# Differential attention in the first block: where the difference of the two softmaxes is formed

## The chip, the cores and the metric

One core of a Trainium2 chip runs the whole program. The metric is the device time of one execution in microseconds (us); the time of the kernel before is the median of three executions.

## The reference, cut to what matters

The model has two blocks one after the other on 256 tokens of width 1024, all in float32. The first block has two layers, each with a feed-forward part, a mixer (a convolution branch, a pooling branch and an attention branch side by side, joined by an output projection) and another feed-forward part. The second block has a Fourier and a window attention mixer and two mixture-of-experts layers. The change is in the attention branch of the first block's mixer, "differential attention": 4 heads, each with two sets of queries and keys (c = 0, 1), queries in blocks of 128, 256 keys.

```python
s = jnp.einsum("bqhcd,bkhcd->bhcqk", q_blk, k)
s = s - slopes[None, :, None, None, None] * dist
p = jax.nn.softmax(s, axis=-1)
a = p[:, :, 0] - lam * p[:, :, 1]
return jnp.einsum("bhqk,bkhe->bqhe", a.astype(v.dtype), v)
```

The output of each head then goes through an RMS norm (the sub-norm) and, beside the conv and pool branches, into the output projection. lam is one number per layer.

## The kernel before

The kernel is written by hand, engine by engine: each engine has its own program, in order, and they meet at counting semaphores. Weights come in panels of 1 MB: SP issues the loads into four raw slots, ACT rounds each panel to a high part (L1206), DVE forms the low part (L1705), and PE multiplies high and low parts in three products (L660, L661, L662). Matrix products outside of this are in plain f32.

The mixer of layer l is `mix1(l)`, which each of the three engines has in its own version. Its attention part is a loop over i = 0 to 7, which stands for query tile `qt = i // 4` and head `h = i % 4`; the text calls i "head i". Every engine runs the loop with a lag, so that while one engine deals with head i another deals with head i-1:

- PE: `scores(i+1)` (L837, two products of 256 columns with K=64), then `attend(i-1)`. attend waits for `a_ready`, transposes the two 128x128 halves of the difference `a1` into PSUM bank 1 (L846), signals `at_ready`, waits until ACT has copied the result to `at1`, and multiplies `at1` with the values `v1` (L851, the "second product"). At i = 1 the mean of the conv norm follows (L823), at i = 2 its variance (L829), at i = 7 the transposes of the attended rows of query tile 0 (`attended_T`, L862). Those of tile 1 follow behind the loop, then the output projection.
- DVE: `bias_and_max(i)` (L1990 adds the distance bias, L1994 takes the row maxima), then `weights(i-1)`: the reciprocals of the two row sums (L2003), the second one times -lam (L2005), `a1` = first exponentials times the first reciprocal (L2006), and `a1` += second exponentials times the scaled second reciprocal (L2008). A drain stands between dependent instructions. At i = 2 the conv norm is centred (behind the mean), at i = 3 normalised (behind ACT's root of the variance), at i = 5 the low part of the conv and pool outputs is formed (behind ACT's silu), at i = 7 the sub-norm of query tile 0 follows.
- ACT: `exps(i)` (L1384, two exponentials with row sums, into `p1`), then `weights_T(i-1)`, the copy of the transposed weights from PSUM to `at1` (L1390). At i = 3 the root of the variance (L1409) follows the copy, at i = 4 the silu and its rounding (L1416, L1420), at i = 7 the sub-norm's parts (L1394, L1396, L1398). Changes of the function cost a table load.

`p1`, `a1`, `at1`, `s1` and the statistics `m1` are double buffered by i % 2. `ident` is the 128x128 identity among the constants.

Elsewhere in the kernel, in the norms, PE transposes and scales rows by a product with a diagonal matrix: DVE makes the diagonal with `tensor_scalar(diag, ident, rs, rt, mult, mult)` in `diagonals` (L1773), and `norm_T` (L674) runs four products of 128x128 by 128 columns to each signal to ACT, whose first reader is L1252.

Of the kernel before, what the change touches and what calls it, by code (L numbers as in the profile page):

```python
# [22 lines left out]
ALU = mybir.AluOpType  # L23
# [7 lines left out]
P = 128  # L31
# [88 lines left out]
def build(nc, A, out):  # L120
# [9 lines left out]
    R0, R1, R2, R3 = 0, 4096, 4096 + 3072, 4096 + 3072 + 3456  # L130

    with ExitStack() as ctx:
        def sb(name, shape, dt=F32):
            return ctx.enter_context(nc.sbuf_tensor(name, shape, dt))

        def sem(name):
            return ctx.enter_context(nc.semaphore(name))
# [31 lines left out]
        ps = ctx.enter_context(nc.psum_tensor("ps", [P, 8, BANK], F32))  # L169
        psf = ps[:, :, :].rearrange("p b c -> p (b c)")  # L170

        def k(name):
            a, n = CA[name]
            return K[:, a:a + n]

        def w(a, n):
            return W[:, a:a + n]

        ident, tri, iota = k("ident"), k("tri"), k("iota")
# [58 lines left out]
        v1 = w(R3 + 4096, 1024).rearrange("p (t n) -> p t n", t=2)  # L238
        s1 = w(R3 + 5120, 1024).rearrange("p (b n) -> p b n", b=2)
        p1 = w(R0 + 2048, 1024).rearrange("p (b n) -> p b n", b=2)  # L240
        a1 = w(R0 + 3072, 512).rearrange("p (b n) -> p b n", b=2)
        at1 = w(R0 + 3584, 512).rearrange("p (b n) -> p b n", b=2)
        osq = w(R2 + 1024, 512)
        on = w(R2 + 1536, 512)
# [1 line left out]
        lam = sb("lam", [P, 8])  # L246
        m1 = sb("row_stats", [P, 2, 8])
# [147 lines left out]
        a_ready = sem("weights_ready")  # L395
# [80 lines left out]
        def slot(p):  # L476

            return w_hi[:, p % SPLIT, :], w_lo[:, p % SPLIT, :]
# [26 lines left out]
        def hi3(pair):  # L505

            return [v.rearrange("p (k n) -> p k n", k=KD) for v in pair]
# [5 lines left out]
        def T(a, n):  # L513

            return t_hi[:, a:a + n], t_lo[:, a:a + n]
# [141 lines left out]
        def _(pe):  # L657
            def product(dst, a, b, start, stop):

                pe.matmul(dst, a[0], b[0], start=start, stop=False)  # L660
                pe.matmul(dst, a[0], b[1], start=False, stop=False)  # L661
                return pe.matmul(dst, a[1], b[0], start=False, stop=stop)  # L662

            def at(pair, *idx):
                return [v[idx] for v in pair]
# [94 lines left out]
            def mix1(l):  # L760
                n = 4 * l + 1
                p = G0[f"in{l}"]
# [4 lines left out]
                for b in range(2):  # L767
                    pe.wait_ge(w_ready, p + b + 1)
                    for c in range(2):
                        for kk in range(KD):  # L770
                            if b == 0 and c == 0:
                                hT_wait(n, kk)
                            mm = product(ps[:, b, c * 256:(c + 1) * 256],
                                         at(hi3(slot(p + b)), slice(None), kk, slice(c * P, (c + 1) * P)),
                                         T(kk * 256, 256), kk == 0, kk == KD - 1)
# [8 lines left out]
                for grp in range(4):  # L784
                    r = 64 * (grp % 2)
                    for t in range(2):
                        mm = pe.matmul(ps[r:r + 64, 2, (grp // 2) * 256:(grp // 2) * 256 + 256],
                                       up[:, t, grp * 64:(grp + 1) * 64], band[:, t, grp, :],
                                       start=t == 0, stop=t == 1)
# [4 lines left out]
                for c in range(2):  # L794
                    for j in range(TAP_STEPS):
                        for q in range(4):
                            mm = pe.matmul(ps[32 * q:32 * q + 32, 1, c * SEQ:(c + 1) * SEQ], tapw[c][:, q, j, :],
                                           zrep[:, c, q, 4 * j:4 * j + SEQ], start=j == 0, stop=j == TAP_STEPS - 1)
# [4 lines left out]
                for c in range(2):  # L803
                    mm = pe.matmul(ps[:, 2, c * 256:(c + 1) * 256], pool_bd[:, l, c, :], dT[:, c, :],
                                   start=True, stop=True)
                mm.then_inc(pp_ready, 1)

                for i, src in enumerate((qn, kn)):
                    pe.wait_ge(qkn_ready, 2 * l + i + 1)
                    for t in range(2):  # L810
                        for h in range(4):
                            mm = pe.transpose(ps[:, 3 + 2 * i + t, h * P:(h + 1) * P],
                                              src[:, t * 512 + h * P:t * 512 + (h + 1) * P], ident)
# [28 lines left out]
                def attend(i):  # L842
                    qt, h = divmod(i, 4)
                    pe.wait_ge(a_ready, 8 * l + i + 1)
                    for t in range(2):
                        mm = pe.transpose(ps[:, 1, (i % 2) * 256 + t * P:(i % 2) * 256 + (t + 1) * P],  # L846
                                          a1[:, i % 2, t * P:(t + 1) * P], ident)
                    mm.then_inc(at_ready, 1)
                    pe.wait_ge(aT_ready, 8 * l + i + 1)
                    for t in range(2):  # L850
                        mm = pe.matmul(ps[:, (7, 0)[qt], h * P:(h + 1) * P], at1[:, i % 2, t * P:(t + 1) * P],  # L851
                                       v1[:, t, h * P:(h + 1) * P], start=t == 0, stop=t == 1)
                    mm.then_inc(o_ready, 1)
# [12 lines left out]
                for i in range(9):  # L866
                    if i + 1 < 8:
                        scores(i + 1)
                    if i >= 1:
                        attend(i - 1)  # L870
                    if i == 1:
                        mean()
                    if i == 2:
                        variance()
                    if i == 7:
                        attended_T(0)
# [821 lines left out]
        def _(dve):  # L1698
# [236 lines left out]
            def mix1(l):  # L1935
                p = G0[f"in{l}"]
# [60 lines left out]
                def weights(i):  # L1997

                    b = i % 2
                    dve.wait_ge(p_ready, 8 * l + i + 1)  # L2000
                    if i >= 2:
                        dve.wait_ge(at_ready, 8 * l + i - 1)
                    dve.reciprocal(m1[:, b, 4:6], m1[:, b, 2:4])  # L2003
                    dve.drain()
                    dve.tensor_tensor(m1[:, b, 6:7], m1[:, b, 5:6], lam[:, 5:6], ALU.mult)  # L2005
                    dve.tensor_scalar(a1[:, b, :], p1[:, b, 0:256], m1[:, b, 4:5], None, ALU.mult)  # L2006
                    dve.drain()
                    dve.scalar_tensor_tensor(a1[:, b, :], p1[:, b, 256:512], m1[:, b, 6:7], a1[:, b, :],  # L2008
                                             ALU.mult, ALU.add).then_inc(a_ready, 1)

                def sub_norm(qt):
                    dve.wait_ge(osq_ready, 2 * l + qt + 1)
# [16 lines left out]
                for i in range(9):  # L2029
                    if i < 8:  # L2030
                        bias_and_max(i)
                    if i >= 1:
                        weights(i - 1)
                    if i == 2:
                        centre()
                    if i == 3:
                        normalise()
                    if i == 7:
                        sub_norm(0)
                    if i == 5:  # L2040
                        dve.wait_ge(ys_hi, l + 1)
                        rest(t_lo[:, 2048:3072], ystage, t_hi[:, 2048:3072]).then_inc(ys_lo, 1)
# [587 lines left out]
```

## Time and profile before

| | before |
|---|---|
| median of 3 runs | 2835.4 us (2830.19 to 2836.94) |
| profiled execution, own time | 2835.73 us |
| its span, first to last instruction | 2833.9 us |
| mean granted TensorE clock | 0.905 |
| PE matmul, busy | 2350.8 us (83%) |
| DVE, busy | 1057.4 us (37%) |
| ACT, busy | 718.1 us (25%) |

The span is the time of the one execution that was profiled; what the device time has beyond it lies before the first and behind the last instruction. A busy time says how long an engine had an instruction in work. A granted clock of 1.00 means that TensorE ran at 2.4 GHz, 0.50 that it ran at 1.2 GHz, a value between them a mixture of the two over the stretch. The attention loops lie at about 309 to 358 us (layer 0) and 886 to 935 us (layer 1).

### The profile page before, as it was taken

The numbers are of one execution on the slowest core, as the hardware profiler recorded it, in microseconds if no ns is written. First come the engines' busy times: TensorE is split into PE (matmuls) and PEld (weight loads), VectorE is DVE, ScalarE is ACT, GpSimd is POOL, SyncE is SP. The second block draws the span as 40 slices with busy tenths as digits, with TensorE's granted clock in tenths as the row PEclk, the third lists the DMA queues.
The fourth block names the chain that finished last, engine by engine and source line by source line (L and its number), as shares of the span: only waits on it lengthen the run. The fifth ranks groups of instructions, "written<-read, shape, count | busy, mean of one in ns | idle before, by whom it ended". The sixth has DMA issues, their size and how long they took to land.

```text
span 2833.9 us, 35797 instructions
## 1 busy us (share of the span) xinstructions
PE 2350.8 (83%) x13958; PEld 1617.6 (57%) x13958; DVE 1057.4 (37%) x1634; ACT 718.1 (25%) x969; POOL 118.3 (4%) x209
## 2 busy tenths in 40 slices
PE   6999689999997699999678888886569578888885
PEld 5888488888885688887523333332545533333332
DVE  4555645565556355724601000001678500000011
ACT  3334433343344233522100000011335100001000
POOL 0001000000010000000010000001000010000000
PEclk9999789999998799999789998898779789889998
DMA  7765137767752377532279999999410289999997
GB/s 258 268 233 179 60 112 264 263 207 263 259 173 83 101 255 249 179 101 86 75 306 393 396 398 401 400 401 400 136 45 1 89 336 397 397 402 402 399 399 303
DMA packets 248615, 713.60 MB, mean 252 GB/s; under 512 B 24432, under 2 KB 163824, under 8 KB 195056
## 3 DMA queue, kind: packets, MB, share of 16 engines
q1 hardware_dynamic: 213584, 642.82, 61.2%
q10 hardware_dynamic: 25936, 43.20, 4.4%
q0 software_dynamic: 8976, 25.90, 3.1%
q8 instruction: 88, 1.44, 0.2%
q14 instruction: 31, 0.25, 0.0%
HBM read 688.45 MB, written 25.26 MB: 252 GB/s over the span
## 4 chain that ended last, share of the span: by engine, by line
PE 57%; DMA 26%; DVE 7%; issue 3%; ACT 2%; DVEq 2%; SPq 1%; ACTq 1%; POOL 0%; POOLq 0%
DMA raw<-in_w 24%; PE ps L660 13%; PE ps L661 12%; PE ps L662 12%; PE ps L1009 11%; PE ps L674 2%; PE ps L701 2%; DMA shift_cols<-mod_rows 1%; SPq L594 1%; PE ps L1011 1%; DVE w_lo L1705 1%; PE ps L1149 1%; PE ps L1164 1%; DMA raw<-in_ffn_w_up 1%; DMA router_rows<-work 1%
## 5 line engine op out<-in xcount | busy, mean ns | idle before, releaser
L1705 DVE TENSOR_TENSOR w_lo<-raw,w_hi 128x2048 fp32r<-128x2048 f32 x180 | 411.4, 2290 | 429.4 <-ACT w_hi L1206 429.1
L1009 PE MATMUL ps<-raw,work 128*64 128x512 f32 x528 | 330.9, 787 | 163.3 <-DMA raw<-in_w 161.9
L660 PE MATMUL ps<-t_hi,w_hi 128*128 128x256 f32 (+1 forms) x1568 | 455.6, 291 | 5.0 <-DVE w_lo L1705 5.0
L1206 ACT CAST w_hi<-raw 128x2048 fp32r<-128x2048 f32 x180 | 342.4, 1906 | 440.9 <-PE ps L662 423.5
L661 PE MATMUL ps<-t_lo,w_hi 128*128 128x256 f32 (+1 forms) x1568 | 453.8, 289 | 0.0
L662 PE MATMUL ps<-t_hi,w_lo 128*128 128x256 f32 (+1 forms) x1568 | 450.7, 287 | 0.0
L2334 DVE COPY work<-ps 128x512 f32<-128x512 f32 x64 | 44.3, 692 | 934.6 <-PE ps L1027 934.6
L660 PE MATMUL ps<-w_hi,t_hi 128*128 128x256 f32 (+1 forms) x1088 | 350.8, 322 | 23.9 <-DVE t_lo L1784 11.5
L662 PE MATMUL ps<-w_hi,t_lo 128*128 128x256 f32 (+1 forms) x1088 | 351.7, 323 | 0.0
L661 PE MATMUL ps<-w_lo,t_hi 128*128 128x256 f32 (+1 forms) x1088 | 351.6, 323 | 0.0
L1011 PE MATMUL ps<-raw,work 128*64 128x512 f32 x528 | 332.4, 790 | 0.0
L660 PEld LDWEIGHTS ps<-t_hi,w_hi 128*128 128x128 f32 x1568 | 296.2, 189 | 25.0 <-issue 13.2
L1009 PEld LDWEIGHTS ps<-raw,work 128*64 128x64 f32 x528 | 87.7, 176 | 383.7 <-issue 382.0
L662 PEld LDWEIGHTS ps<-t_hi,w_lo 128*128 128x128 f32 x1568 | 297.1, 189 | 4.6
L661 PEld LDWEIGHTS ps<-t_lo,w_hi 128*128 128x128 f32 x1568 | 295.7, 189 | 5.6
L1009 PE MATMUL ps<-work 128*64 128x512 f32 x496 | 229.2, 605 | 17.3 <-DMA work<-in_w 17.2
L660 PEld LDWEIGHTS ps<-w_hi,t_hi 128*128 128x128 f32 x1088 | 212.1, 195 | 40.4 <-DVE t_lo L1784 11.7
L1011 PE MATMUL ps<-work 128*64 128x512 f32 x496 | 229.5, 606 | 0.0
L1027 PE MATMUL ps<-raw,work 128*64 128x512 f32 x992 | 226.7, 598 | 0.2 <-DMA raw<-in_w 0.2
L1550 ACT COPY work<-ps 128x512 f32<-128x512 f32 x64 | 37.5, 586 | 715.3 <-PE ps L1011 715.3
L662 PEld LDWEIGHTS ps<-w_hi,t_lo 128*128 128x128 f32 x1088 | 210.2, 193 | 14.1
L661 PEld LDWEIGHTS ps<-w_lo,t_hi 128*128 128x128 f32 x1088 | 210.1, 193 | 13.4
(317 smaller groups left out, 2222.2 us busy)
## 6 DMA issues: line engine op xcount, KB each, us to landing
raw<-in_w SPq DMA_DIRECT2D x256, 1024.0 KB, 11.2
work<-in_w SPq DMA_DIRECT2D x128, 1024.0 KB
work<-in_w_mod SPq DMA_DIRECT2D x32, 1536.0 KB, 6.4
raw<-in_ffn_w_gate SPq DMA_DIRECT2D x44, 1024.0 KB, 8.8
raw<-in_ffn_w_up SPq DMA_DIRECT2D x44, 1024.0 KB, 9.7
raw<-in_ffn_w_down SPq DMA_DIRECT2D x44, 1024.0 KB, 5.0
raw<-in_w_in SPq DMA_DIRECT2D x18, 1024.0 KB, 5.4
expert_rows<-work ACTq DMA_DIRECT2D x128, 128.0 KB, 7.3
```

The costliest lines, as they stand in the source:

```text
L660: pe.matmul(dst, a[0], b[0], start=start, stop=False)
L661: pe.matmul(dst, a[0], b[1], start=False, stop=False)
L662: return pe.matmul(dst, a[1], b[0], start=False, stop=stop)
L674: mm = pe.matmul(ps[:, norm_bank(n, s) + j, q * P:(q + 1) * P], norm_source(n)[:, t, kk * P:(kk + 1) * P], diag(n)[:, t, :], start=True, s ...
L701: mm = pe.matmul(ps[32 * q:32 * q + 32, bank + a // BANK, 0:n], cond[:, kk, :], mod_raw[:, q * MOD_Q + a:q * MOD_Q + a + n], start=True, s ...
L1009: first = pe.matmul(ps[0:BLK, 2 + par, :], xT[:, par, kk * BLK:(kk + 1) * BLK], w1[:, j * BANK:(j + 1) * BANK], start=kk == 0, stop=kk == ...
L1011: mm = pe.matmul(ps[BLK:P, 2 + par, :], xT[:, par, kk * BLK:(kk + 1) * BLK], w3[:, j * BANK:(j + 1) * BANK], start=kk == 0, stop=kk == KD - 1)
L1027: mm = pe.matmul(ps[BLK * half:BLK * half + BLK, 6 + par, :], am[:, par, c * BLK:(c + 1) * BLK], w2[:, j * D + half * BANK:j * D + (half + ...
L1206: act.copy(slot(j)[0], src).then_inc(w_hi_ready, 1)
L1550: act.copy(gusb[:, par, :], ps[:, 2 + par, :]).then_inc(gu_ready, 1)
L1705: return dve.tensor_tensor(dst, src, hi.bitcast(F32), ALU.subtract)
L2334: dve.tensor_copy(ysb[:, par, :], ps[:, 6 + par, :]).then_inc(y_copied, 1)
```

## The change

The difference is no longer formed on DVE. DVE makes two diagonal matrices from the identity, one with the first reciprocal sums and one with the second reciprocal sums times -lam, and PE multiplies the exponentials with them, adding the two products in PSUM. As the exponentials are the stationary operand, the result comes out transposed, as the transposes gave it. `a1` goes away, and `d1`, with two diagonals for each i % 2, takes its place in memory.

```diff
-        a1 = w(R0 + 3072, 512).rearrange("p (b n) -> p b n", b=2)
+        d1 = w(R0 + 3072, 512).rearrange("p (b c n) -> p b c n", b=2, c=2)
...
                     pe.wait_ge(a_ready, 8 * l + i + 1)
                     for t in range(2):
-                        mm = pe.transpose(ps[:, 1, (i % 2) * 256 + t * P:(i % 2) * 256 + (t + 1) * P],
-                                          a1[:, i % 2, t * P:(t + 1) * P], ident)
+                        for c in range(2):
+                            mm = pe.matmul(ps[:, 1, (i % 2) * 256 + t * P:(i % 2) * 256 + (t + 1) * P],
+                                           p1[:, i % 2, c * 256 + t * P:c * 256 + (t + 1) * P], d1[:, i % 2, c, :],
+                                           start=c == 0, stop=c == 1)
                     mm.then_inc(at_ready, 1)
...
                     dve.reciprocal(m1[:, b, 4:6], m1[:, b, 2:4])
                     dve.drain()
-                    dve.tensor_tensor(m1[:, b, 6:7], m1[:, b, 5:6], lam[:, 5:6], ALU.mult)
-                    dve.tensor_scalar(a1[:, b, :], p1[:, b, 0:256], m1[:, b, 4:5], None, ALU.mult)
-                    dve.drain()
-                    dve.scalar_tensor_tensor(a1[:, b, :], p1[:, b, 256:512], m1[:, b, 6:7], a1[:, b, :],
-                                             ALU.mult, ALU.add).then_inc(a_ready, 1)
+                    dve.tensor_scalar(d1[:, b, 0, :], ident, m1[:, b, 4:5], None, ALU.mult)
+                    dve.tensor_scalar(d1[:, b, 1, :], ident, m1[:, b, 5:6], lam[:, 5:6], ALU.mult, ALU.mult).then_inc(a_ready, 1)
```

## Rows read from the trace of the kernel before

**Rows 1.** The page, its first line.
```profile
span 2833.9 us, 35797 instructions
```
**Rows 2.** Chain of waits, 300 to 380: start us, us, engine, tile, line.
```profile
315.21 0.70 PE ps L846 x2
...
317.58 1.72 PE ps L823 x4
...
323.33 0.45 PE ps L846 x2
...
333.27 0.70 PE ps L846 x2
...
345.66 0.70 PE ps L846 x2
...
355.42 0.70 PE ps L846 x2
...
364.92 0.55 PE ps L660
...
370.81 0.21 PE ps L662
371.02 0.12 PE ps L660
```
**Rows 3.** Windows: stretch, length, busy time (count) of each engine, PE clock, DMA share, GB/s.
```profile
315.00:320.00 5.00, 4.33 (x14) 2.82 (x14) 3.09 (x8) 1.61 (x7) 0.00 (x0) 0.53 0.01 3
...
340.00:345.00 5.00, 3.94 (x14) 2.65 (x14) 3.31 (x10) 2.50 (x10) 0.00 (x0) 0.50 0.00 0
```
**Rows 4.** Timeline (start us, us, engine, line), layer 1, head 7, 925 to 948.
```profile
932.66 0.69 PE L846 MATMUL ps<-consts,work 128*128 128x128 f32 x2 [2.54 <-DVE work L2008]
```
**Rows 5.** Timeline, layer 0, head 3, weights to second product.
```profile
332.00 0.15 DVE L2003 RECIPROCAL row_stats<-row_stats 128x2 f32<-128x2 f32 x1
...
332.22 0.16 DVE L2005 TENSOR_TENSOR row_stats<-row_stats,lam 128x1 f32<-128x1 f32 x1
...
332.73 0.48 DVE L2008 SCALAR_TENSOR_TENSOR work<-work,row_stats 128x256 f32<-128x256 f32 x1
...
333.27 0.69 PE L846 MATMUL ps<-consts,work 128*128 128x128 f32 x2 [7.69 <-DVE work L2008]
...
334.00 0.37 ACT L1390 COPY work<-ps 128x256 f32<-128x256 f32 x1 [0.79 <-PE ps L846]
...
334.42 1.22 PE L851 MATMUL ps<-work 128*128 128x128 f32 x4 [0.46 <-ACT work L1390]
```
**Rows 6.** Timeline, 605 to 613, the norm ahead of layer 1's first feed-forward part.
```profile
604.97 0.60 DVE L1773 TENSOR_SCALAR work<-consts,rstd,rstd_error 128x128 f32<-128x128 f32 x2
605.63 5.64 PEld L674 LDWEIGHTS ps<-work 128*128 128x128 f32 x32 [7.47 <-DVE work L1773]
...
607.74 0.84 ACT L1252 ACTIVATE t_hi<-ps,gain_cols 128x256 fp32r<-128x256 f32 x2 [3.78 <-PE ps L674]
```
**Rows 7.** Timeline, layer 0, head 1, at full clock.
```profile
320.07 0.44 PE L846 MATMUL ps<-consts,work 128*128 128x128 f32 x2
...
320.55 0.37 ACT L1390 COPY work<-ps 128x256 f32<-128x256 f32 x1 [2.91 <-PE ps L846]
...
320.97 0.71 PE L851 MATMUL ps<-work 128*128 128x128 f32 x4 [0.46 <-ACT work L1390]
```
**Rows 8.** Timeline, layer 0, heads 4 and 5.
```profile
336.73 0.69 PE L846 MATMUL ps<-consts,work 128*128 128x128 f32 x2
...
340.19 0.35 ACT L1390 COPY work<-ps 128x256 f32<-128x256 f32 x1
...
340.60 1.22 PE L851 MATMUL ps<-work 128*128 128x128 f32 x4 [3.18 <-ACT work L1390]
...
341.75 1.23 PE L837 MATMUL ps<-work 64*128 64x256 f32 x4
...
342.90 0.69 PE L846 MATMUL ps<-consts,work 128*128 128x128 f32 x2
```

## The prediction

> **What bounds the kernel now.** I read the page first for the span [rows 1], then the chain of waits between 300 and 380 us (the first layer's attention and the start of its out-projection), then the granted clock by windows and the timeline of the same stretch, engine by engine. In the chain the reader sees a ladder of short steps on which DVE, PE and ACT relieve each other: the two transposes of L846 stand on it five times a layer, for heads 0, 2, 3, 6 and 7 of the eight; the five rows are those of L846 [rows 2]. No DMA moves meanwhile (share 0.00 in 340 to 345 [rows 3]): the weight slots are full, and everything later waits for this layer's residual, so what the ladder gains or loses is carried to the end. The second layer repeats the first: head 7's transposes take 0.70 us from 355.42 in the one and 0.69 from 932.66 in the other [rows 2, 4]. I work out one layer and double it.
>
> **The DVE leg.** Before, 1.27 us pass from the reciprocal's start (332.00) to the transposes' start (333.27) [rows 5]. After, the reciprocal and its drain stay (0.22, to 332.22), then come two scalings of the 128x128 identity. The kernel has such a pair, L1773, in each norm: 0.60 us for two, each with two scalars, and PE starts 0.06 behind [rows 6]. Together 0.88 us: 0.39 less a head. One of the new two has a single scalar and may be shorter. Bounds for the pair: 0.60, and as little as the 0.48 that the one instruction L2008 takes [rows 5], as the pair writes no more elements. I take 0.60, the row of the same operation.
>
> **The PE leg.** Before, two transposes, one record each; ACT's copy starts 0.73 us after the first at 1.2 GHz (333.27 to 334.00) [rows 5] and 0.48 after it at 2.4 GHz (320.07 to 320.55) [rows 7]. After, four f32 products of 128 columns, c=0 and c=1 for each half of the keys. An f32 product leaves two records (the two of L851 appear as four [rows 5]), so eight. L674 in the norms is exactly this, data as weights, a diagonal moving, four products to a signal: ACT starts 2.11 us after the first (605.63 to 607.74) at 1.2 GHz [rows 6]. **Added: 1.38 us a head.** At 2.4 GHz no row shows it alone. Four records of L851 take 1.22 at 1.2 GHz and 0.71 at 2.4 [rows 5, 7]; eight at 1.2 GHz 2.07 (the 2.11 less the 0.04 by which ACT's start lags behind PE's end [rows 5]), which is 0.85 of twice 1.22, so I take 0.85 of twice 0.71, 1.2 us. **Added: 0.72.** Bounds 0.71 and 1.42 for the eight, so 0.23 and 0.94 added.
>
> One rule speaks against this edit. The Trainium skill, "TensorE: Matmul & The Clock Gate", section "Terms", says that the transpose mode is 4 times faster for FP32. By that alone four products would cost eight times two transposes, over 5 us a head at 1.2 GHz, and a layer would lose some 20 us. L674's row gives 2.11, under three times the 0.73, much of which is latency; the row decides.
>
> **The sum for a layer,** as lateness against before.
> Head 0: -0.39 on DVE, +1.38 on PE: its copy comes 1.0 late. Its second product and then the mean of the conv norm (L823, on the chain [rows 2]) follow on PE, and DVE waits for that mean.
> Heads 1 and 2: PE runs scores, first and second products and the variance without a pause, so its own length counts and DVE's 0.39 is worth nothing: +0.72 twice, at 2.4 GHz. Against it, the clock rose at about 319.7 before (granted 0.53 in 315 to 320 [rows 3]); the mean now begins 1 us later, so its last part and scores 3 fall into 2.4 GHz: -0.5, an estimate from its 1.72 on the chain [rows 2], of which a half would go if all of it ran at 2.4 GHz. Copy 2 is 1.9 late. In ACT's program the root of the variance stands behind that copy, and on DVE the normalisation behind the root, then bias 4 and weights 3: all 1.9 late.
> Head 3: PE long idle, at 1.2 GHz: +1.0, so 2.9. The silu of the conv branch stands behind copy 3 on ACT, exps 5 behind the silu.
> Head 4: covered. Its transposes start at 336.73, its copy only at 340.19, after exps 5 [rows 8]: 2.7 us of cover for 1.4 more. Without it, 1.4 us on the ladder.
> Heads 5 and 6: after copy 4 PE runs head 4's second product, scores 7, head 5's transposes (340.60, 341.75, 342.90 [rows 8]), head 5's second product, and head 6's transposes at 345.66 [rows 2]. All at 1.2 GHz this is +1.38 for head 5, of which 0.4 disappears in the gap before head 6 (that gap was DVE's weights 6), and +1.38 for head 6: +2.4. If the clock has risen by the end of head 5's four products, its second product is 0.5 shorter and head 6's four 0.9 shorter than at 1.2 GHz, which leaves +1.0, and the longer f32 work of scores 7 and head 5 may run partly at 2.4 GHz too (up to 0.5 more). I take +0.5. The reason: today PE works there in stretches of 3 us (340.60 to 343.6), in part with transposes, at a granted 0.50 [rows 3, 8]; after the change it works from copy 4 on for 8 us with gaps of 0.4 only, longer than the 6 us of the out-projection from 364.92 to 371.0 after which the clock rose (0.21 us a product before, 0.12 after [rows 2]). So 3.4.
> Head 7: behind the sub-norm, PE idle before, 1.2 GHz: +1.0. **4.4 us a layer, 8.8 in all.**
> The profiled run took 2835.73 us, of which 2833.9 is span [rows 1]; it becomes 2844.5. It stands 0.3 above the median of the runs shown, 2835.4; so 2844.
>
> No wait is added by name. p1 is now read by PE, and its next writer, exps i+2 on ACT, already stands behind copy i; that copy comes later, and exps 2 with it, but weights 2, which need them, wait for the mean. POOL and SP have no part in it.
>
> **Rivals.**
> *A. The clock stays at 1.2 GHz in the whole second half* (0.25), as today. Heads 5 and 6 cost 2.4: 6.3 a layer, 6.8 without the 0.5 from the mean: 2848 to 2849.
> *B. The clock, once up after head 3, stays up: not slower* (0.10). The place is PE from copy 4 to the out-projection. From 2.9: second product of head 4 and scores 7 -0.5 each (1.22 to 0.71; 1.15 by the starts 341.75 and 342.90 [rows 8], likewise nearly halved), weights 6 -0.39, head 6 +0.5 (1.2 for 0.73): 2.0. Then the sub-norm's two sets of four transposes -0.4 each, head 7 +0.1 (1.2 for 0.73, less 0.39), its second product -0.5: 0.8. The 6 us of the out-projection at 0.21 for 0.12 give back 2.6: -1.8 a layer, 2832; with half of the projection's gain 2834.5. It turns the sign if the clock survives the 2 us idle before copy 4 and the 4 us in the sub-norm. Against it: after heads 1 and 2 it fell and was at 1.2 GHz for head 3 [rows 5, 7], though after 8 us idle. For it: the Trainium skill, same page, Part 4 "PE-mode transpose", says that a transpose does not count as PE-busy for the clock as a product does, so this exchange adds more activity than its length. Heads 3 to 6, with transposes among products, stayed at 0.50 [rows 3], which agrees, but no run here separates the two.
> *C. A rise that comes earlier than I say* (0.20), for head 5 already, or for most of the mean: 1.3 to 3 a layer, 2838 to 2841.
> *D. Not on the ladder* (0.02): ACT released after one pair of products, nothing lost: 2835.
> My forecast, 2842 to 2847 with the spread of the moment of the rise, has 0.43.
>
> **The numbers.** 0.3% is 8.5 us, about what a measurement of this kernel can tell from no change; the forecast sits on that line. Slower by more: A and a good half of the forecast, 0.52. Within: the rest of it, C, D, most of B, 0.43. Faster by more needs B with the mean at 2.4 GHz too (another -1 a layer): 0.05. The range reaches from B's mild end and C, 2836, to A with 2 us for a later rise in the projection, 2851.
>
> **What would show it.** Right: 128 records in place of L846's 32; ACT's copy 2.1 us after the first of them in heads 0, 3 and 7 and 1.2 in heads 1 and 2; the two scalings 0.60 together, PE 0.88 after the reciprocal's start; measured from the first bias, the mean's successor 1.0 or less late, the normalisation 1.9, silu 2.9, out-projection 4.4, in both layers; copy 4 still behind exps 5. Wrong: a granted clock that rises between heads 3 and 7 at another place than with head 6 (A, B, C), eight records at 2.4 GHz off 1.2 us, or PE idle before head 2, which would mean that DVE and not PE ends last there.

## The result, and the profile after

| | before | after |
|---|---|---|
| median | 2835.12 us (6 runs) | 2846.36 us (2842.41 to 2850.07, 6 runs) |
| ratio to before | | 1.0041, 95% interval 1.0028 to 1.0054 |
| span of the profiled execution | 2833.9 us | 2848.2 us |

The change costs 0.41%, 11.6 us by the ratio, with an interval from 7.9 to 15.3. Forecast were 8.8 us (2844, range 2836 to 2851). The sign is as forecast, and the 8.8 lie inside the interval near its lower end.

The page of the changed kernel, first line, busy times, and the row of the clock in 40 slices:

```profile
span 2848.2 us, 35957 instructions
...
PE 2346.7 (82%) x14054; PEld 1634.9 (57%) x14054; DVE 1051.5 (37%) x1618; ACT 717.4 (25%) x969; POOL 119.9 (4%) x209
...
PEclk9999889999998899999779998898779789989998
```

PE has 96 matmul records more (128 in place of 32), DVE 16 instructions less and 5.9 us less to do; the shares say nothing of the 11 us. The timeline of layer 0 does. Head 3 (start us, us, engine, line; compare [rows 5]):

```profile
335.07 0.15 DVE L2005 RECIPROCAL row_stats<-row_stats 128x2 f32<-128x2 f32 x1
...
335.31 0.29 DVE L2007 TENSOR_SCALAR work<-consts,row_stats 128x128 f32<-128x128 f32 x1
335.51 0.34 DVE L2008 TENSOR_SCALAR work<-consts,row_stats,lam 128x128 f32<-128x128 f32 x1
...
335.90 2.08 PE L847 MATMUL ps<-work 128*128 128x128 f32 x8 [7.24 <-DVE work L2008]
...
338.01 0.37 ACT L1392 COPY work<-ps 128x256 f32<-128x256 f32 x1 [1.73 <-PE ps L847]
```

From the reciprocal to PE's start 0.83 us pass (before 1.27), from PE's start to ACT's copy 2.11 (before 0.73): 0.44 gained on DVE, 1.38 lost on PE. Head 1, at 2.4 GHz (compare [rows 7]):

```profile
321.94 1.16 PE L847 MATMUL ps<-work 128*128 128x128 f32 x8
...
323.13 0.37 ACT L1392 COPY work<-ps 128x256 f32<-128x256 f32 x1 [3.61 <-PE ps L847]
```

1.19 us to the copy against 0.48 before. Heads 4 to 6 (compare [rows 8]), with the second products L853 and scores L837:

```profile
340.75 2.07 PE L847 MATMUL ps<-work 128*128 128x128 f32 x8
...
344.21 0.35 ACT L1392 COPY work<-ps 128x256 f32<-128x256 f32 x1
...
344.61 1.22 PE L853 MATMUL ps<-work 128*128 128x128 f32 x4 [1.79 <-ACT work L1392]
...
345.76 1.23 PE L837 MATMUL ps<-work 64*128 64x256 f32 x4
...
346.92 1.86 PE L847 MATMUL ps<-work 128*128 128x128 f32 x8
...
349.24 0.71 PE L853 MATMUL ps<-work 128*128 128x128 f32 x4 [0.46 <-ACT work L1392]
...
349.79 1.06 PE L847 MATMUL ps<-work 128*128 128x128 f32 x8
```

The reader sees head 4 covered (its eight records end at 342.82, its copy waits for exps 5 until 344.21), and the clock change inside head 5: 1.86 us for eight records, then 0.71 for four and 1.06 for eight. The windows of the same stretch, the next to last three numbers of which are PE clock, DMA share and GB/s (compare [rows 3]), show where it rises and that it has fallen again for head 7:

```profile
340.00:345.00 5.00, 3.21 (x14) 2.27 (x13) 2.92 (x6) 4.91 (x11) 0.00 (x0) 0.50 0.01 2
345.00:350.00 5.00, 4.54 (x22) 3.47 (x22) 2.19 (x6) 1.83 (x9) 0.00 (x0) 0.66 0.00 0
350.00:355.00 5.00, 1.55 (x12) 1.17 (x10) 1.92 (x8) 2.62 (x6) 0.00 (x0) 1.00 0.00 0
355.00:360.00 5.00, 1.63 (x6) 1.26 (x7) 2.37 (x6) 0.59 (x1) 0.00 (x0) 0.52 0.00 0
```

The steps of the ladder, each as its start less the start of the layer's first bias instruction (L1990, after: L1992; 311.20 and 888.11 before, 312.49 and 893.08 after):

| step | layer 0 before, after | late | layer 1 before, after | late | forecast |
|---|---|---|---|---|---|
| DVE centres (behind the mean) | 8.13, 8.92 | 0.79 | 8.46, 8.76 | 0.30 | 1.0 or less |
| DVE normalises (behind copy 2 and the root) | 14.80, 16.59 | 1.79 | 15.14, 16.43 | 1.29 | 1.9 |
| low part behind the silu (behind copy 3) | 26.72, 29.44 | 2.72 | 27.05, 29.28 | 2.23 | 2.9 |
| sub-norm of tile 0 (behind copy 6) | 36.09, 39.29 | 3.20 | 36.43, 39.05 | 2.62 | 3.4 |
| sub-norm of tile 1 (behind head 7) | 47.26, 51.40 | 4.14 | 47.59, 51.15 | 3.56 | 4.4 |
| last step before the out-projection | 52.93, 57.43 | 4.50 | 53.27, 56.83 | 3.56 | 4.4 |

Two of the steps hold a pause on DVE in which, by the profile, it waits for nobody (the row says "issue"). The changed kernel has one in layer 0, in the second sub-norm, which makes up the 0.36 us of the last step. The kernel before has one in layer 1, in head 0's weights; its transposes start 4.34 us behind the first bias there, in layer 0 4.01:

```profile
366.09 0.17 DVE L1722 TENSOR_SCALAR rstd_error<-rstd_error 128x4 f32<-128x4 f32 x1 [0.42 <-issue]
```

```profile
891.47 0.35 DVE L2006 TENSOR_SCALAR work<-work,row_stats 128x256 f32<-128x256 f32 x1 [0.24 <-issue]
```

Both repeat. The first is in layer 0 of all seven traces in which DVE makes the diagonals (after, e0, e10, e1, e4, e6, e7) and in none of the other seven. The second is in all three traces of the kernel before and in none of the changed one. So some 0.7 us of the difference between the two layers' 4.50 and 3.56 comes from these pauses and not from PE. What causes them is not shown.

### The profile page after: what moved, and what is told of

Read it like the earlier page. It is cut to its first block, busy times and chain, and to the rows that moved or that the text cites. A ratio compares the mean times of both kernels' runs of the same rounds, so it can differ in the third digit from the quotient of the medians.

```text
span 2848.2 us, 35957 instructions
## 1 busy us (share of the span) xinstructions
PE 2346.7 (82%) x14054; PEld 1634.9 (57%) x14054; DVE 1051.5 (37%) x1618; ACT 717.4 (25%) x969; POOL 119.9 (4%) x209
## 4 chain that ended last, share of the span: by engine, by line
PE 57%; DMA 27%; DVE 7%; issue 3%; ACT 2%; DVEq 2%; SPq 1%; ACTq 1%; POOL 0%; POOLq 0%
DMA raw<-in_w 24%; PE ps L660 13%; PE ps L661 12%; PE ps L662 12%; PE ps L1011 11%; PE ps L674 2%; PE ps L701 2%; DMA shift_cols<-mod_rows 1%; SPq L594 1%; PE ps L1013 1%; PE ps L847 1%; PE ps L1151 1%; DVE w_lo L1707 1%; PE ps L1166 1%; DMA raw<-in_ffn_w_up 1%
## 5 line engine op out<-in xcount | busy, mean ns | idle before, releaser
L1011 PE MATMUL ps<-raw,work 128*64 128x512 f32 x528 | 310.3, 745 | 169.5 <-DMA raw<-in_w 168.1
L660 PE MATMUL ps<-w_hi,t_hi 128*128 128x256 f32 (+1 forms) x1088 | 351.7, 323 | 23.9 <-DVE t_lo L1707 10.5
L1013 PE MATMUL ps<-raw,work 128*64 128x512 f32 x528 | 311.9, 748 | 0.0
L1029 PE MATMUL ps<-raw,work 128*64 128x512 f32 x992 | 226.5, 598 | 0.0
```

The source lines that it names most:

```text
L1011: first = pe.matmul(ps[0:BLK, 2 + par, :], xT[:, par, kk * BLK:(kk + 1) * BLK], w1[:, j * BANK:(j + 1) * BANK], start=kk == 0, stop=kk == ...
L1013: mm = pe.matmul(ps[BLK:P, 2 + par, :], xT[:, par, kk * BLK:(kk + 1) * BLK], w3[:, j * BANK:(j + 1) * BANK], start=kk == 0, stop=kk == KD - 1)
L1029: mm = pe.matmul(ps[BLK * half:BLK * half + BLK, 6 + par, :], am[:, par, c * BLK:(c + 1) * BLK], w2[:, j * D + half * BANK:j * D + (half + ...
```

## The experiments

Each ratio is to runs of the kernel before on the same chip. What I call the loop is the stretch from the first bias to the last step of the table above; the out-projection stretch runs from there to the last of the residual additions; the tail is everything behind those of layer 1. These lengths come from one trace each. A row without a ratio is a single execution, run for its trace:

| kernel | loop 0 | loop 1 | out-proj. 0, 1 | tail | ratio to before (95%) |
|---|---|---|---|---|---|
| before | 52.93 | 53.27 | 26.6, 26.4 | 1866.1 | |
| e8_before_again | 52.94 | 53.29 | 26.5, 26.4 | 1864.1 | |
| e9_before_third | 52.93 | 53.27 | 26.5, 26.4 | 1873.0 | |
| after | 57.43 | 56.83 | 26.2, 26.3 | 1872.0 | 1.0041 (1.0028 to 1.0054) |
| e0_changed | 56.98 | 56.83 | 26.1, 26.3 | 1865.3 | 1.0042 (1.0028 to 1.0055) |
| e10_changed_third | 57.20 | 56.84 | 26.1, 26.3 | 1872.1 | |
| e1_dve_alone | 51.44 | 51.35 | 25.7, 26.0 | 1873.2 | 0.9994 (0.9985 to 1.0003) |
| e2_pe_alone | 58.60 | 59.47 | 25.3, 25.4 | 1867.3 | 1.0047 (1.0033 to 1.0061) |
| e3_two_products | 55.35 | 55.68 | 25.6, 25.6 | 1866.6 | 1.0012 (1.0003 to 1.0021) |
| e4_eight_products | 66.14 | 66.02 | 25.4, 25.6 | 1871.6 | 1.0092 (1.0076 to 1.0107) |
| e5_fill_before | 50.26 | 50.07 | 23.9, 23.9 | 1861.1 | 0.9965 (0.9951 to 0.9978) |
| e6_fill_after | 52.38 | 52.16 | 23.9, 23.9 | 1862.5 | 0.9972 (0.9961 to 0.9983) |
| e7_early_first | 57.64 | 56.40 | 26.2, 26.5 | 1873.5 | 1.0031 (1.0019 to 1.0044) |
| e11_fill_out | 52.43 | 52.84 | 23.9, 25.3 | 1860.3 | 0.9987 (0.9978 to 0.9996) |

**The changed kernel again, and both kernels for more traces** (e0_changed, e8_before_again, e9_before_third, e10_changed_third; no edit).

> The changed kernel again, unedited. Theory (the PE leg of the products is longer than the transposes by 1.4 us at 1.2 GHz and 0.7 at 2.4, less 0.39 on DVE, on the ladder of the first block's attention): 8 to 9 us over the kernel before, with 4.5 and 3.6 us added between the first bias and the out-projection of the two layers of its first trace. Rival (something outside the two attention loops also became slower, since the first profiled execution is 14 us longer with only 8 of them in the loops): 11 us or more again, and again a part of it behind the first block.

> The kernel before, unedited, for a second trace. Theory (the added time lies in the two attention loops and nothing outside them changed): 52.5 to 53.5 us from the first bias to the last sub-norm step in both layers, 496 to 500 us between the layers' loops, and what follows the first block anywhere between 1860 and 1874 us, as in the traces of the edited kernels. Rival (the changed kernel also slows what follows the first block): 1862 to 1868 again, under the changed kernels.

> The same once more: the same numbers, to see how far the stretch behind the first block moves between executions of one kernel.

> The changed kernel once more. Theory: 56.5 to 57.5 us a loop, 3.5 to 4.5 over before, with the clock at 1.2 GHz for head 5's start and at 2.4 by head 6; behind the first block 1860 to 1874. Rival: 1870 or more behind the first block, as in its first trace.

e0: median 2845.74 us against 2834.67, ratio 1.0042, 11.9 us (7.9 to 15.6); the 8 to 9 expected lie inside the interval, near its lower end. The loops repeat to 0.02 us in the kernel before and to 0.45 in the changed one, so their difference is sure: 3.6 to 4.5 us each, 7.6 to 8.1 for both. The tail, whose code the change doesn't touch, took 1864.1, 1866.1 and 1873.0 us in three executions of the kernel before and 1865.3, 1872.0 and 1872.1 in three of the changed one. The two sets overlap, so the 14.3 us by which the first pair of spans differed were in the main 8 of loops and 6 of a tail that moves by 9 in the unchanged kernel too. The rival's form that every execution of the changed kernel has a tail of 1870 or more fell with e0. Its weaker form stands: e0's total was over 11 us again, as the rival had it, and over all traces the seven in which DVE makes the diagonals have a mean tail of 1870.0 us (1862.5 to 1873.5), the other seven 1865.5 (1860.3 to 1873.0). A difference of 4.5 us between sets that each spread over 11 to 13 is not shown to be real, and no run tests it.

**The DVE leg alone** (e1). It leaves out the second softmax.

```diff
-                          a1[:, i % 2, t * P:(t + 1) * P], ident)
+                          p1[:, i % 2, t * P:(t + 1) * P], ident)
...
+                    dve.tensor_scalar(d1[:, b, 0, :], ident, m1[:, b, 4:5], None, ALU.mult)
+                    dve.tensor_scalar(d1[:, b, 1, :], ident, m1[:, b, 5:6], lam[:, 5:6], ALU.mult, ALU.mult).then_inc(a_ready, 1)
```

> Leaves out the second softmax and the scaling of the first: DVE makes the two diagonals, which nobody multiplies with, and PE transposes the raw exponentials of c=0 as two transposes. So it has the new DVE leg with the old PE leg. Theory: 0.39 us less for heads 0, 3, 6 and 7, where DVE ends last before the transposes, 1.2 to 1.6 a layer, 2 to 3 us less than the kernel before in all, and no change of the clock. Rival (the diagonals are no cheaper for what follows, as PE or ACT end last): within 0.5 us of before.

Measured: the loops are 1.49 and 1.92 us shorter, 3.4 together; the ratio of 0.9994 (minus 1.7 us, interval minus 4.3 to plus 0.9) can't tell this from nothing, its trace does. Head 3:

```profile
331.57 0.15 DVE L2003 RECIPROCAL row_stats<-row_stats 128x2 f32<-128x2 f32 x1
...
332.40 0.69 PE L846 MATMUL ps<-consts,work 128*128 128x128 f32 x2 [7.25 <-DVE work L2006]
...
333.13 0.37 ACT L1390 COPY work<-ps 128x256 f32<-128x256 f32 x1 [0.35 <-PE ps L846]
```

0.83 and 0.73: the new DVE leg with the old PE leg. What follows: DVE's part is on the ladder, 0.44 us for each of four heads a layer (0, 3, 6 and 7), 1.8 in all. Beside it, the two pauses shift the loops: layer 0 gains one (1.84 us shorter at the second sub-norm, 1.49 at the end), layer 1 loses one. The 3.4 are a little more than the 2 to 3 expected, which had reckoned 0.39 for three to four heads.

**The PE leg alone** (e2). It computes twice the difference, which the norm behind it takes out again but for its epsilon.

```diff
-                        mm = pe.transpose(ps[...], a1[:, i % 2, t * P:(t + 1) * P], ident)
+                        for c in range(2):
+                            mm = pe.matmul(ps[...], a1[:, i % 2, t * P:(t + 1) * P], ident, start=c == 0, stop=c == 1)
```

> Computes twice the difference: DVE forms it as before, and PE multiplies each half twice with the identity in four f32 products, so it has the old DVE leg with the new PE leg. Theory: 1.38 us more for heads 0, 3 and 7 (0.39 more each than in the changed kernel), the same for heads 1, 2 and about the same for 5 and 6: 5.6 to 6 a layer between the first bias and the out-projection, 11 to 12 us over before. Rival (the DVE leg is not on the ladder): as the changed kernel, 8 to 9.

Measured: loops +5.67 and +6.20, 11.9 together, out-projections -2.3; ratio 1.0047, 13.3 us (9.4 to 17.3). The copy of head 3 starts 2.11 us after PE here too:

```profile
333.74 2.08 PE L847 MATMUL ps<-consts,work 128*128 128x128 f32 x8 [7.70 <-DVE work L2010]
...
335.85 0.37 ACT L1392 COPY work<-ps 128x256 f32<-128x256 f32 x1 [2.18 <-PE ps L847]
```

The two halves nearly add up: -3.4 and +11.9 in the loops make 8.5, the whole change 7.6 to 8.1. In layer 0 they do (4.18 against 4.05 to 4.50). In layer 1 they give 4.28 against 3.56, and 0.6 of that 0.7 arises between the silu and the sub-norm of tile 0, where the clock rises later in e2 than in the changed kernel: head 5's eight records take 2.07 us and head 6's 1.36, against 1.77 and 1.06.

**Two products in place of two transposes** (e3).

```diff
-                        mm = pe.transpose(ps[...], a1[:, i % 2, t * P:(t + 1) * P], ident)
+                        mm = pe.matmul(ps[...], a1[:, i % 2, t * P:(t + 1) * P], ident, start=True, stop=True)
```

> As the kernel before, but each transpose is an f32 product with the identity: two products, four records, in place of two. Theory: from L851's four records, the copy starts 1.26 us after the first at 1.2 GHz against 0.73, so +0.53 for heads 0, 3, 5 in part, 6 and 7, +0.27 for heads 1 and 2 at 2.4 GHz: 2.2 a layer, 4 to 5 us in all, with the clock in the second half of the loop at 1.2 GHz still, as the stretches without a gap hardly grow. Rival (a transpose does not count as activity for the clock, a product does): the clock rises in heads 4 to 6, and the total is within 2 us of before.

Measured: loops +2.42 and +2.41, 4.8 together, ratio 1.0012 (+3.4 us, 0.9 to 6.0). The clock in the second half of loop 0:

```profile
335.00:340.00 5.00, 4.29 (x15) 3.12 (x16) 2.46 (x7) 3.58 (x7) 0.00 (x0) 0.50 0.00 0
340.00:345.00 5.00, 2.36 (x11) 1.60 (x9) 3.49 (x7) 4.11 (x11) 0.00 (x0) 0.50 0.00 2
345.00:350.00 5.00, 4.08 (x17) 2.93 (x13) 2.36 (x6) 2.00 (x7) 0.00 (x0) 0.50 0.00 0
350.00:355.00 5.00, 1.25 (x5) 0.98 (x6) 2.98 (x9) 1.89 (x3) 0.00 (x0) 0.50 0.00 0
```

It stays at 1.2 GHz through heads 3 to 7, although no transpose is left in the heads (the four of the sub-norm remain). So exchanging transposes for products did not by itself lift the clock here; with four products a head, in the same places (e2 and the changed kernel), it did rise. The Trainium skill's sentence, in "TensorE: Matmul & The Clock Gate", Part 4, that a transpose does not count as PE-busy as a product does, had spoken for a rise here; no run shows one.

**Twice the PE leg** (e4): `for c in (0, 1, 0, 1)` in place of `for c in range(2)`; start and stop go by c as before, so the second pair computes the same difference again.

> The changed kernel with the four products of each head run twice (eight products, sixteen records; the second set overwrites the first, the result is the same). Theory (the PE leg is what costs): at 1.2 GHz 8 records of 0.213, 1.7 us more for heads 0, 3 and 7; 0.9 more for heads 1 and 2 at 2.4 GHz; head 4 no longer covered (0.4 more), heads 5 and 6 at 2.4 GHz from an earlier point, 0.5 to 0.9 more each: 7 to 9 a layer over the changed kernel, 14 to 18 in all. Rival (PE has room, and the waits cost): under 6 in all.

Measured: ratio 1.0092, 26.1 us over before, 14.5 over the changed kernel by the ratios; loops +8.7 and +9.2 over it, 17.9. At the upper end of what the theory gave for the loops. Head 3 takes 3.52 us for sixteen records where two times the eight would be 4.2, since the clock rises in it:

```profile
337.81 3.52 PE L847 MATMUL ps<-work 128*128 128x128 f32 x16 [7.24 <-DVE work L2008]
...
341.79 0.71 PE L853 MATMUL ps<-work 128*128 128x128 f32 x4 [0.46 <-ACT work L1392]
```

**An earlier start for the first product** (e7).

```diff
-                    pe.wait_ge(a_ready, 8 * l + i + 1)
                     for t in range(2):
                         for c in range(2):
+                            if t == 0:
+                                pe.wait_ge((d0_ready, a_ready)[c], 8 * l + i + 1)
...
-                    dve.tensor_scalar(d1[:, b, 0, :], ident, m1[:, b, 4:5], None, ALU.mult)
+                    dve.tensor_scalar(d1[:, b, 0, :], ident, m1[:, b, 4:5], None, ALU.mult).then_inc(d0_ready, 1)
```

> The changed kernel with its own semaphore for the first diagonal, so that the first of the four products starts while DVE makes the second. Theory: DVE's second scaling ends 0.25 us behind the first, so 0.25 less for heads 0, 3 and 7 and perhaps 6: 0.75 to 1 a layer, 1.5 to 2 us in all below the changed kernel, still over the kernel before. Rival (two waits cost PE more than the overlap gives): no change.

Measured: ratio 1.0031, overlapping the changed kernel's 1.0041; loops 57.64 and 56.40 against 56.98 to 57.43 and 56.83. Inconclusive in the whole. In layer 1, where the clock changes in the same places as in the changed kernel, the loop is 0.43 shorter, half of what was expected: heads 3 and 7 give 0.25 each, head 0 0.12 behind the mean, and heads 5 and 6 take 0.2 back. Head 3 shows the overlap itself, 0.57 us from the reciprocal to PE against 0.83:

```profile
334.61 0.15 DVE L2007 RECIPROCAL row_stats<-row_stats 128x2 f32<-128x2 f32 x1
...
335.18 2.08 PE L849 MATMUL ps<-work 128*128 128x128 f32 x8 [6.99 <-DVE work L2009]
...
340.03 1.83 PE L849 MATMUL ps<-work 128*128 128x128 f32 x8
...
345.39 2.07 PE L849 MATMUL ps<-work 128*128 128x128 f32 x8
```

In layer 0 the clock rose already in head 4 (1.83 us), where nobody waits, and had fallen again in head 5 (2.07, which the ladder pays). A saving of 0.25 us a head is smaller than what the moment of a clock change moves. Whether the earlier start moved the rise in layer 0, one trace can't say.

**Filler for the clock** (e5 in the kernel before, e6 in the changed one, e11 in one place of the kernel before).

```diff
+                def busy(n, bank=0):
+                    for _ in range(n):
+                        pe.matmul(ps[:, bank, 384:512], ones[:, :], K[:, 0:128], start=True, stop=True)
...
+                    busy({3: FILL3, 7: FILL7}.get(i, 0))
                     pe.wait_ge(a_ready, 8 * l + i + 1)
...
                     mm.then_inc(at_ready, 1)
+                    if i == 4:
+                        busy(FILL4)
...
                 def attended_T(qt):
+                    busy(FILL[qt], 7 * qt)
```

Products of constants go into PSUM columns that nobody has in use. Counts (FILL3, FILL4, FILL7, FILL): e5 28, 10, 9, (15, 18); e6 28, 10, 8, (15, 18); e11 0, 0, 0, (0, 10).

> The kernel before with products of the constants into PSUM columns that nobody reads, in the places where PE waits: 28 before head 3, 10 before head 4's second product, 15 and 9 in and behind the first sub-norm, 18 in the second, sized to end before the wait does at 2.4 GHz. Theory (rival B of the prediction: the low clock costs the ladder and the start of the out-projection): the clock stays at 1.00 from head 2 to the out-projection, the ladder is 3 to 3.5 shorter a layer and the out-projection 2.6: 10 to 12 us less than before. Rival (the clock falls in spite of it, or the filler runs at 1.2 GHz and ends after the wait): 0 to 5 us more than before, seen as PE rows of the filler that end behind the releaser.

> The same filler in the changed kernel. Theory: with a high clock the exchange costs 0.7 less 0.39 for heads 3 and 7, 0.7 for 1, 2 and 5 in part, so 2 to 3 us a layer over the filled kernel before instead of 4.4: 4 to 6 over it, and 5 to 7 under the kernel before without filler. Rival (the clock has no part): as the changed kernel or slower.

> The kernel before with filler products in one place only, ten behind head 7's second product, while PE waits for the second sub-norm: 4.3 us at 1.2 GHz, 4.6 us of wait. Theory (of the 11 us that the full filler gave, 5 lie in the start of the out-projection, the rest in the loop): the ladder up to head 7 is as before, the out-projection runs at 2.4 GHz from its start or soon after, 1.5 to 2.6 a layer, 3 to 5 us in all. Rival (4 us of filler is too little for the clock to rise by then): under 1 us a layer.

Measured: e5 0.9965, 9.9 us under before (6.2 to 13.9); loops -2.67 and -3.20, out-projections -2.65 and -2.47, 11.0 together. e6 0.9972, 7.9 us under before. e11 0.9987, 3.7 us under before (1.1 to 6.2); 0.9 in the loops, 3.7 in the out-projections. Against the expectations: e11 lies inside its 3 to 5, e5 at the lower edge of 10 to 12 by the ratio, and e6 is somewhat more under before (7.9, interval 4.8 to 11.1) than the 5 to 7 named. The second out-projection of e11 gave only 1.1 of its 3.7, as the clock was at about 0.65 from 939 to 944. e5, layer 0: the filler before head 3, the transposes behind it, and the clock:

```profile
325.38 6.52 PE L862 MATMUL ps<-consts,ones 128*128 128x128 f32 x56
...
333.15 0.44 PE L848 MATMUL ps<-consts,work 128*128 128x128 f32 x2 [1.25 <-DVE work L2018]
```

```profile
335.00:340.00 5.00, 3.06 (x26) 2.48 (x22) 2.89 (x5) 4.90 (x10) 0.00 (x0) 1.00 0.00 2
340.00:345.00 5.00, 2.86 (x16) 1.75 (x16) 3.46 (x11) 2.98 (x11) 0.00 (x0) 1.00 0.02 3
345.00:350.00 5.00, 4.84 (x28) 4.85 (x29) 2.98 (x9) 2.18 (x4) 0.00 (x0) 0.66 0.00 0
350.00:355.00 5.00, 4.00 (x34) 3.57 (x33) 1.67 (x5) 0.96 (x2) 0.00 (x0) 1.00 0.01 2
```

The filler before head 3 ends 1.25 us before the transposes are released. In the first sub-norm of layer 0 the rival of e5 came true in part: the clock fell at about 346.4, 0.7 us into the filler, and was back at 1.00 only from 349.8. The same thirty records took 5.14 us, in layer 1 at 2.4 GHz 3.51:

```profile
345.70 5.14 PE L862 MATMUL ps<-consts,ones 128*128 128x128 f32 x30
```

There they end behind the releaser (DVE is done at 349.99, the sub-norm's transposes start at 350.68), and the step from the sub-norm of tile 0 to that of tile 1 takes 10.47 us, in layer 1 9.94. In the other loops of e5 and e6 the clock stays at 1.00 from head 1 on.

What the exchange costs with the clock held high is the difference of e6 and e5: 2.09 us in layer 1, and in layer 0 2.12, or 2.65 if those 0.53 us are left out of e5, of which 0.35 are the pause. So of the 3.6 to 4.5 us a layer, 1.4 to 1.9 are there only because PE runs part of the loop at 1.2 GHz. e5 is quicker than both kernels; against e6 its loops are shorter by 2.1 us each, while the two ratios overlap.

## Why the prediction was right, point by point

**The ladder and its carrying to the end**: right in direction and in the main in size. e5 has 11.0 us in the stretches against 9.9 by the ratio, e2 9.6 (11.9 less 2.3) against 13.3, both inside their intervals. The changed kernel has 7.5 against 11.6 (7.9 to 15.3) and e1 -4.7 against -1.7 (-4.3 to 0.9): both just outside, and both higher in the whole than in the stretches.

**The DVE leg**: -0.39 forecast, -0.44 measured (0.83 from the reciprocal to PE). The instruction with one scalar takes 0.29 us, not 0.34, and the next starts 0.20 behind it. I had named this and taken the longer value.

**The PE leg**: 2.11 us at 1.2 GHz as in the norms' row, measured 2.11 [rows 6]; 1.2 at 2.4 GHz from the factor 0.85, measured 1.19. The FP32 factor of 4 of the Trainium skill ("TensorE: Matmul & The Clock Gate", "Terms") does not describe this: the four products cost 2.9 times the two transposes to the copy, and e3's two products take 1.26 us where the transposes took 0.73.

**Heads 0 to 3**: 1.9 and 2.9 forecast; 1.79 and 2.72 in layer 0, 1.29 and 2.23 in layer 1. By ACT's copies and the start of head 1's products, layer 0 first, layer 1 second: head 0 +0.94 and +0.60 (1.0 forecast), the mean and scores 3 -0.36 and -0.32 (-0.5), head 1 +0.71 in both (0.72), head 2 +0.50 and +0.31 (0.72), head 3 +0.93 and +0.94 (1.0). The mean's term was about right in both layers. Layer 1 is short because of head 0: before, its DVE leg held the pause at 891.47, 0.33 us that the prediction, which compared the layers by head 7's transposes alone, did not see. Head 2 was mis-sized in both: before, PE was not busy without a pause there, as the step says, but waited for DVE's weights (L2008 ends at 323.28, the transposes start at 323.33, scores 3 had ended at 323.18). That layer 0 came out near 1.9 all the same is in part luck: the mean was to give back 0.14 too much and head 2 to cost 0.22 too much, and the two errors nearly cancel.

**Head 4 covered, heads 5 and 6 +0.5**: right, in both layers: +0.48 in layer 0 and +0.39 in layer 1 (from the silu row to the sub-norm row of the table), +0.32 and +0.39 in e0. The clock rose inside head 5, as the step assumed; in the kernel before it stayed at 0.50, so rival A fell. The parts are less exact than the sum: head 5's eight records gave back 0.2 (1.86 us for 2.07) and scores 7 nothing (1.23), where up to 0.5 was taken for them, and head 6's copy came 1.09 behind its first record and not 1.2. It is the step with the least ground, and e3 shows how near it was to the other side: with two products a head in place of four no rise came, while in four executions with four (after, e0, e2, e10) the windows of 345 to 350 show 0.64 to 0.83. In e7, also with four, it rose in head 4 and was at 0.50 in that window.

**Head 7, 1.2 GHz, +1.0**: +0.94 in both layers.

**Rival B** had the right price and did not happen by itself: the clock fell again in the sub-norm (0.52 in 355 to 360). e5 and e6 made it happen with filler. For the changed kernel that is 7.9 us under before, more than the 3 to 4 that I had worked out. The filler begins earlier than the rival's high clock: up to the silu e6 is only 1.5 us late, where the rival starts from 2.9.

**The total**: 8.8 forecast, 7.6 to 8.1 in the loops, the two out-projections together 0.6 shorter, so 7.0 to 7.5 in these stretches. The medians show 11, the two ratios 11.6 and 11.9 with lower bounds of 7.9. The rest, some 4 us, is not in the rows of the change; the tail moves by 9 us between executions of one kernel, and the traces with diagonals have the longer tails on average. Whether the change lengthens the tail stays open. The prediction put everything outside the loops at nothing, and no run shows that this is so.

## What to carry to other kernels

Look at which engine ends last at each rung before moving work off a less busy one: here DVE was busy for 37% and PE for 83% of the time, DVE gave up 0.44 us a head, and PE took 1.38 for the same head. A price for a new instruction can often be read from a place where the kernel already runs the same one; the norms' diagonal products gave 2.11 us to the hundredth. And where short dependent steps leave PE idle, ask at what clock it runs: 1.4 to 1.9 of the 3.6 to 4.5 us that the exchange cost a layer hung on that, and filler products in the waits of the old kernel took 10 us off. And read both layers before doubling one: a pause of 0.3 us on DVE that stood only in layer 1 is 0.33 of the 0.84 us by which the forecast missed that layer (4.4 against 3.56).

## What the runs showed of the hardware

The traces repeat. In three executions of the kernel before, loop 0 took 52.93, 52.94 and 52.93 us, with the clock changes in the same places, while everything behind the first block's last mixer took 1864 to 1873.

Taking transposes away did not raise the clock (e3, 0.50 from 335 to 355). In the one trace of e7 the clock rose in layer 0 in head 4 and not in head 5, and fell again before it could help; in layer 1 of the same trace it rose in head 5.

Filler that runs in waits costs nothing where it ends before the releaser. The granted clock stayed at 1.00 through waits of up to 1.9 us between bursts (e5, before head 4's second product). But in layer 0 of e5 it fell at about 346.4. PE had worked without a pause since 345.16, and before that, from 338.3 on, in short pieces with waits of up to 1.9 us. In layer 1, behind the same pieces, it did not fall. So filler sized for 2.4 GHz can end too late, as it did there by 0.5 us.

DVE has pauses of 0.24 and 0.42 us that stand in the same place in every execution of a kernel and vanish or appear when its program gets three instructions where it had four (before, L2006 in layer 1; after, L1722 in layer 0).
